# Two transformer blocks on one core: the output projection's first weights in free ring slots, the queries' weights split on VectorE alone, both attentions' preparation at other steps

## What is computed

```python
def gdn_mixer(h, w_in, conv_w, a_log, dt_bias, out_gain, w_out):
    proj = h @ w_in
    qkv = jax.nn.silu(causal_dwconv(proj[..., :GDN_CONV_DIM], conv_w))
    q, k = l2_norm(q), l2_norm(k)
    o = gated_delta_rule(tr(q), tr(k), tr(v), tr(g), tr(beta))
    o = o * rsqrt(mean(o * o)) * out_gain * jax.nn.silu(z)
    return o @ w_out
```

```python
pa, pb, pc, pd = _split(h @ w_in[l], GROUP_COLS)
ya = _rwkv7_mixer(pa, ...)
yb = _diff_attn_mixer(pb, ...)          # rms_norm and rope of q and k, two softmaxes, p1 - lam * p2
yc = _spatial_gating_mixer(pc, ...)     # gelu, layer_norm, matmul with a triangular matrix
yd = _forgetting_attn_mixer(pd, ...)    # rms_norm of q and k, softmax with a cumulated log gate
x = x + g1 * (concatenate([ya, yb, yc, yd]) @ w_out[l])
h = _rms_norm(x, norm2_g[l]) * (1.0 + sc2) + sh2
x = x + g2 * _conv_glu_ffn(h, ...)
```

## Time and profile before

| | us |
|---|---|
| median of 3 runs | 1643.72 |
| lowest and highest | 1641.59, 1648.09 |
| the profiled execution | 1640.39 |
| its span, first to last instruction | 1638.6 |
| mean granted clock of TensorE | 0.966 |

### The profile page before, as it was taken

One profiled execution on the slowest core, in us unless ns is written; L12 is line 12 of the kernel. 1 busy time (PEld: TensorE's weight loads), 2 busy tenths in 40 slices (PEclk: granted clock), 3 DMA queues, 4 the chain that ended last, 5 costly groups with the idle time before them and its releaser, 6 DMA issues.

```text
span 1638.6 us, 35397 instructions
## 1 busy us (share of the span) xinstructions
PE 1545.2 (94%) x15328; PEld 1402.4 (86%) x15328; DVE 1091.1 (67%) x1790; ACT 886.0 (54%) x1456; POOL 410.3 (25%) x276
## 2 busy tenths in 40 slices
PE   6998998899999989999999898999999989999999
PEld 6988888689998887999888777899988778799987
DVE  5664564357879767687987766776646665676664
ACT  7554563345444555644446565566635763566652
POOL 2243352233443100154322330012200131012220
PEclk9999999999999999999999989999999986999999
DMA  7322210537889443588872302555452400455550
GB/s 282 110 99 79 80 53 5 233 128 286 332 321 355 160 158 122 217 337 330 334 273 85 121 4 101 215 199 172 164 180 69 151 27 28 174 187 172 189 180 26
DMA packets 40188, 275.90 MB, mean 168 GB/s; under 512 B 4576, under 2 KB 4832, under 8 KB 8672
## 3 DMA queue, kind: packets, MB, share of 16 engines
q1 hardware_dynamic: 40032, 273.63, 45.2%
HBM read 272.57 MB, written 1.05 MB: 167 GB/s over the span
## 4 chain that ended last, share of the span: by engine, by line
PE 79%; DVE 8%; ACT 7%; issue 2%; DMA 2%; POOL 1%; ACTq 0%; SPq 0%; DVEq 0%; POOLq 0%
PE ps L554 22%; PE ps L556 21%; PE ps L555 21%; PE ps L562 3%; DVE wl L542 2%; PE ps L567 2%; DMA ring<-in_ws 1%; ACT wh L534 1%; PE ps L2203 1%; ACT ps L773 1%; PE ps L974 1%; PE ps L1095 0%; PE ps L2989 0%; DVE x_sb L3016 0%; PE ps L2586 0%
## 5 line engine op out<-in xcount | busy, mean ns | idle before, releaser
L542 DVE TENSOR_TENSOR wl<-ring,wh 128x1024 fp32r<-128x1024 f32 (+4 forms) x371 | 472.8, 1281 | 309.7 <-ACT wh L534 307.3
L534 ACT ACTIVATE wh<-ring 128x1024 fp32r<-128x1024 f32 (+4 forms) x428 | 436.5, 1027 | 407.8 <-PE ps L556 395.3
L554 PE MATMUL ps<-hTh,wh 128*128 128x256 f32 (+1 forms) x1912 | 551.7, 289 | 7.4 <-DVE hTl L711 3.5
L556 PE MATMUL ps<-hTh,wl 128*128 128x256 f32 (+1 forms) x1912 | 544.3, 285 | 1.3 <-issue 1.3
L555 PE MATMUL ps<-hTl,wh 128*128 128x256 f32 (+1 forms) x1912 | 542.0, 283 | 0.0
L554 PEld LDWEIGHTS ps<-hTh,wh 128*128 128x128 f32 (+1 forms) x1912 | 364.0, 190 | 14.7 <-DVE wl L542 5.8
L555 PEld LDWEIGHTS ps<-hTl,wh 128*128 128x128 f32 (+1 forms) x1912 | 365.2, 191 | 0.5 <-issue 0.2
L556 PEld LDWEIGHTS ps<-hTh,wl 128*128 128x128 f32 (+1 forms) x1912 | 362.2, 189 | 1.5 <-issue 1.5
L550 POOL TENSOR_TENSOR wl<-ring,wh 128x1024 fp32r<-128x1024 f32 x57 | 154.4, 2708 | 398.4 <-ACT wh L534 398.4
L1502 DVE SCALAR_TENSOR_TENSOR arena<-arena 128x1024 f32<-128x1024 f32 x96 | 166.8, 1754 | 0.9 <-DMA arena<-in_ws 0.9
L554 PE MATMUL ps<-wh,acts 128*128 128x512 f32 x366 | 145.1, 396 | 0.0
(11 more groups left out here) (470 smaller groups left out, 2149.0 us busy)
## 6 DMA issues: line engine op xcount, KB each, us to landing
ring<-in_ws SPq DMA_DIRECT2D x197, 1024.0 KB, 5.1
arena<-in_ws SPq DMA_DIRECT2D x48, 1024.0 KB, 8.6
ring<-in_ws SPq DMA_DIRECT2D x5, 768.0 KB, 4.5
ring<-in_ws SPq DMA_DIRECT2D x4, 512.0 KB, 3.7
ring<-in_ws SPq DMA_DIRECT2D x2, 780.0 KB, 4.3
rowt<-in_rowp SPq DMA_DIRECT2D x2, 610.0 KB, 5.0
x_sb<-in_x SPq DMA_DIRECT2D x2, 512.0 KB, 4.6
arena<-in_rowp SPq DMA_DIRECT2D x2, 512.0 KB, 6.6
```

The lines of the kernel that those rows point to most:

```text
L534: ac.act(unit_hl(u)[0], unit_src(u), ACT.Copy).then_inc(*W.a(("hi", u)))
L542: ve.tt(l, unit_src(u), h, OP.subtract).then_inc(*W.v(("lo", u)))
L554: pe.mm(o_, lh, rh, start=start, stop=False)
L556: return pe.mm(o_, ll, rh, start=False, stop=stop)
```

## The change

Three edits in one diff. The pieces of the queries and keys lose their second argument, so no unit of theirs goes to GpSimd. The output projection's loads no longer begin at turn 4, they count on from v and z. In the mixers the differential attention's preparation begins at 19 instead of 17, the forgetting attention's at 29.5 instead of 32.5, and the lambda vectors' products stand at 2.5 instead of 2.

```diff
-    groups = [("ba", pieces_tok("ba", 0, 8, 32), None), ("qk", pieces_T("qk", QKORDER, 8, 3), [0, 1, 2, 3]), ("vz", pieces_vz(), [0, 1, 2, 3]), ("go", pieces_N("go", 16, 3), None)]
+    groups = [("ba", pieces_tok("ba", 0, 8, 32), None), ("qk", pieces_T("qk", QKORDER, 8), [0, 1, 2, 3]), ("vz", pieces_vz(), [0, 1, 2, 3]), ("go", pieces_N("go", 16, 3), None)]
...
     for name, pieces, slots in groups:
-        if name == "go":
-            turn = 4
         if name in ("win0", "win1", "pj00", "pj10", "wo0", "wo1"):
             turn = 0
...
-        MIXT = dict(rw=3.5, rw_by=1.6, mat_by=1.76, inv_by=1.1, out_by=1.76, df0=17.0, df0_by=0.765, fx0=32.5, fx0_by=0.938, sg=3.8, sg_by=0.618, df1=31.0, df_gap=5.0, df_by=1.1, fx1=47.5, fx_gap=1.5, fx_by=1.0, wof=13.0, pjo=-1.0, dot=2.0)
+        MIXT = dict(rw=3.5, rw_by=1.6, mat_by=1.76, inv_by=1.1, out_by=1.76, df0=19.0, df0_by=0.765, fx0=29.5, fx0_by=0.938, sg=3.8, sg_by=0.618, df1=31.0, df_gap=5.0, df_by=1.1, fx1=47.5, fx_gap=1.5, fx_by=1.0, wof=13.0, pjo=-1.0, dot=2.5)
```

## The result

| | before | changed |
|---|---|---|
| median, us (14 runs each) | 1646.97 | 1638.26 |
| lowest and highest, us | 1635.7, 1652.51 | 1628.94, 1645.53 |
| the profiled execution, us | 1640.39 | 1634.65 |
| its mean granted clock | 0.966 | 0.973 |

The ratio is 0.9958, with a 95% interval of 0.9938 to 0.9978: about 6.9 us less (the two medians lie 8.7 us apart). The interval leaves out 1, but the gain is under the 0.5% that the prediction had set as its bound for "faster". I had forecast 9.7 us less. The total was near, but by parts it was wrong: the 7.4 us of part 1 did not come, part 2 cost a little, and part 3, which I gave 1.8 us, brought nearly everything. The experiments show this; the profile of the changed kernel already hints at it.

The account below looks back on a forecast made before the run. TensorE, busy in every slice, was taken to bound the kernel. Gains of 7.4, 0.5 and 1.8 us summed to 9.7 us, taking the median from 1643.7 to 1634.0 us; the forecast's range was 1630 to 1639.

Parts of the forecast that it names:

- part 1: At the output projection's weights: loads into free ring slots remove the 6.0 us gap behind L1223; 7.4 us gained.
- part 2: Queries' and keys' weights, split on VectorE alone: tiny operations ahead of L857 get shorter, one split stands ahead; 0.5 us gained.
- part 3: Both mixers, the attentions' preparation moved: 0.5 - 1.0 + 1.4 = 0.9 us per mixer, 1.8 us gained for both.
- The whole 5.98 us goes: Before the output projection: TensorE's idle gap behind L1223 vanishes entirely, as early loads have landed before their splits; 5.98 us.
- Rival C: The gap before the output projection only shrinks, as the inverse's chain comes late: 3.0 instead of 7.4 us, 1638.4; chance 0.10.
- The hand-over to the second block: After the second feed-forward: the next group's first loads come some 17 us later, from 842.09, and cost nothing, at most 5 us.
- the second tiny operation: L857, right behind L854 in the queries' and keys' stretch: shortened about as much as L854's 0.87 us, 1.7 us together.
- The copies' gap: In each mixer, TensorE's wait before the last projection block for the copy at L1983: 0.5 us shorter, bounds 0 to 4.57.
- The first head's wait: In each mixer, TensorE waits for eight copies before the first head's scores: 1.0 us lost, bounds 0 to 3.0.
- what the forgetting attention gives back: In each mixer's inverse, ScalarE loses two table loads, 2.6 us; 1.4 us gained per mixer, bounds 0 to 2.6.
- rival B: The second mixer's long slow-clock stretch ends as the first's does: 8.9 us more gained, 1625; chance 0.31.
- rival D: TensorE waits 3.0 us per mixer for the eight copies and the first mixer's clock stays low: 1651; chance 0.07.

Follow-up runs that it names:

- e1_go: The kernel before with only the output projection's ring slots changed, so three loads go out early; ratio 0.9997 (0.9975 to 1.0018).
- e4_spare: The kernel before with three spare 1 MB loads into free ring slots 1 to 3, read by nothing; ratio 1.0043 (1.0025 to 1.0062).
- e5_hold: The kernel before with the splits of the output projection's first three units two half steps later, no load moved; ratio 0.9963 (0.9941 to 0.9985).
- e6_hold_mix: The kernel before with the output projection's first splits later and the mixers' preparation moved; ratio 0.9921 (0.9893 to 0.9948), median 1631.94 us.

## Why the prediction was right in sum and wrong in its parts

- **Part 1, 7.4 us: wrong, about 0.5 us (minus 3 to plus 4) by e1_go's ratio.** The steps of the mechanism held: slots free, loads before 285, no wait of ScalarE for the landing, the gap gone. The failed step is "The whole 5.98 us goes", put into the sum with no term for what the moved loads cost: I worked out what the slots' turn does at the hand-over, and put at nothing, without a reason, what three loads of 1 MB meet at 230 to 260 us. The same three loads without a moved split cost 7 us (e4_spare). The sign that I had named, the output projection's matmuls 7 us earlier, did not come: 1.5 us earlier in e1_go, 2.8 later in the changed kernel. The rows were there. I had set the 13.7 us of "issue" aside as something that "waits for nothing that the profile shows", when the DMA view shows the queue it waits for. The gap was sized well by what e5_hold gained, 6.1 us. Rival C's time was near for another reason: the gap did not shrink, it went, and its gain was spent elsewhere. That is two effects, of 6 us by e5_hold and of 7 by e4_spare, that cancel as far as the runs can tell (3 to 4 us).
- **The hand-over to the second block: right.** The changed kernel's offset is the same, +1.3 us, at 667, 860 and 896 us, though the group's loads now go out from 843.27 on, as I had said.
- **Part 2, plus 0.5 us: wrong in sign, about minus 1.** The step that failed is that the second tiny operation would shorten "about as much": it took 0.91 us instead of 0.96, so 0.9 us were gained and not 1.7, against the split's 1.2. The wait of 0.5 us for L1002, 23 us later, had no term.
- **Part 3, single terms.** The copies' gap gave 1.05 us a mixer (forecast 0.5, df0's). The first head's wait costs 0.85 (forecast 1.0). Two table loads a mixer went, as forecast. The middle of 1.4 us for what the forgetting attention gives back did not show as less waiting: TensorE's idle time in the mixers rose by 2.5 us, 2.7 of it behind L2680, a wait that I did not name.
- **Part 3, the sum, 1.8 us: too small by 5.** By its ratio it is worth 6.9 us. The direction was in rival B: the second mixer's long stretch was cut from 30.7 to 13.7 us. I had taken one execution's first mixer for the rule, so I saw only one stretch to gain from, and thought the first could be lost (rival D). D, E and F did not happen. I had written that I am wrong if either mixer changes by over 5 us, and by that sign I was: between the two profiles the second one got 5.9 us shorter (106.7 to 100.8). Which step failed is known, that the clock of both mixers was taken to stay as one profile had it; why it falls less stays open.
- So the time fell inside of the range because an error of 7 us in part 1 and one of 5 us the other way in part 3 nearly cancel, not because the reasons held. That is luck.

## What to carry to other kernels

Before a transfer is moved ahead, look at what TensorE does in its new place: a run of small matmuls lives on its instruction fetches, and a weight load in front of one costs more than it looks. If an engine waits for a load that can't come earlier, move the work that waits behind the next urgent step, not the load. And do not size anything by the clock of one profile: the same instructions took 114 to 124 us in one stretch here, over seven executions, so compare stretches over several executions.

## What the runs showed of the hardware

- "issue" before small matmuls is the wait for 16 KB of TensorE's instructions: 56 of 56 gaps of 0.9 us and over end 1.2 to 1.6 us after such a packet has landed. The packet takes about 1 us itself, and behind a ring load of 1 MB, whose packets take 3.4 us, it started as these end in five of six cases.
- The place at which the clock falls differs between executions of the same instructions: the stretch of 7 us at 41 us in one execution (e6_hold_mix) is one of 3.4 us at 34 us in another (e5_hold), and up to there the two kernels are the same.
- A VectorE operation of 128 x 32 took 0.19 us with GpSimd idle, and 0.91 to 1.10 us where it stood beside a GpSimd operation and ended with it (25 of 28 in the 14 traces; the other three, each right behind a VectorE split, took 0.18 to 0.19). The Trainium skill, SBUF, State Buffer ("SBUF: two separate sides"), has this as an exclusive lock between the two; the trace agrees, and it holds for a product of GpSimd of 512 columns as for a split.
